# Rotary halves of queries and keys: 32 small transfers issued by ScalarE in place of eight permutation products on TensorE

## What is computed

```python
qkv = (x @ w_qkv).reshape(B, T, 3, H, Dh)
q = apply_rope(q, cos, sin) * (Dh ** -0.5)
k = apply_rope(k, cos, sin)

def apply_rope(t, cos, sin):
    t1, t2 = jnp.split(t, 2, axis=-1)
    return jnp.concatenate([t1 * cos - t2 * sin, t2 * cos + t1 * sin], axis=-1)

s_own = jnp.where(causal, einsum('bhqd,bhsd->bhqs', q_c, k_own), -jnp.inf)
p = softmax(s_own); out = (p @ v) @ w_o
```

## Time and profile before

| | us |
|---|---|
| median of 3 runs | 1294.86 (1294.64 to 1295.3) |
| the profiled execution | 1294.79 |
| its span | 1292.9 |
| TensorE busy | 1246.3 (96%) |
| VectorE busy | 902.7 (70%) |
| ScalarE busy | 641.3 (50%) |
| GpSimd busy | 69.7 (5%) |
| chain that ended last | PE 72%, DVE 19%, ACT 7%, issue 2% |

### The profile page before, as it was taken

One profiled execution on the slowest core, in us unless ns is written; L12 is line 12 of the kernel. 1 busy time (PEld: TensorE's weight loads), 2 busy tenths in 40 slices (PEclk: granted clock), 3 DMA queues, 4 the chain that ended last, 5 costly groups with the idle time before them and its releaser, 6 DMA issues.

```text
span 1292.9 us, 22010 instructions
## 1 busy us (share of the span) xinstructions
PE 1246.3 (96%) x9332; PEld 1087.3 (84%) x9332; DVE 902.7 (70%) x1433; ACT 641.3 (50%) x966; POOL 69.7 (5%) x43
## 2 busy tenths in 40 slices
PE   6999999999999999999999999999999999999997
PEld 4788898788888888768888889999898987788886
DVE  7456885766655677756665568989999766665555
ACT  3433445464554455556444445444455556555553
POOL 0022000002000061000200010000000000000000
PEclk9999999999999999999999999999999999999999
DMA  9532201665655374326555537455544343355550
GB/s 306 174 110 77 87 4 52 212 231 192 197 195 195 106 245 172 120 77 228 196 195 196 194 112 233 131 163 184 161 145 162 132 163 106 122 202 191 193 180 33
DMA packets 156211, 205.97 MB, mean 159 GB/s; under 512 B 9904, under 2 KB 129840, under 8 KB 155984
## 3 DMA queue, kind: packets, MB, share of 16 engines
q1 hardware_dynamic: 156112, 204.55, 47.9%
HBM read 202.44 MB, written 1.05 MB: 157 GB/s over the span
## 4 chain that ended last, share of the span: by engine, by line
PE 72%; DVE 19%; ACT 7%; issue 2%; DMA 0%; DVEq 0%; SPq 0%; ACTq 0%
PE PS L591 15%; PE PS L543 11%; PE PS L544 11%; PE PS L545 11%; PE PS L596 8%; DVE WW L2157 6%; PE PS L961 4%; DVE PH L2748 4%; ACT WW L1519 2%; PE PS L892 1%; DVE PA L2396 1%; PE PS L932 1%; ACT Xb L1555 1%; PE PS L668 1%; DVE PH L2766 1%
## 5 line engine op out<-in xcount | busy, mean ns | idle before, releaser
L2157 DVE TENSOR_TENSOR WW<-RG,WW 128x2048 fp32r<-128x2048 f32 x164 | 381.0, 2337 | 141.9 <-ACT WW L1519 141.7
L1519 ACT ACTIVATE WW<-RG 128x2048 fp32r<-128x2048 f32 x164 | 311.1, 1906 | 27.6 <-PE PS L545 24.8
L591 PE MATMUL PS<-AHL,WW 128*128 128x512 f32 x864 | 216.9, 392 | 0.4 <-DVE WW L2157 0.4
L543 PE MATMUL PS<-AHL,WW 128*128 128x256 f32 x704 | 203.3, 289 | 2.5 <-DVE AHL L2196 1.8
L544 PE MATMUL PS<-AHL,WW 128*128 128x256 f32 x704 | 199.1, 283 | 0.0
L545 PE MATMUL PS<-AHL,WW 128*128 128x256 f32 x704 | 199.1, 283 | 0.0
L591 PEld LDWEIGHTS PS<-AHL,WW 128*128 128x128 f32 x864 | 157.1, 189 | 30.0 <-DVE WW L2157 0.8
L543 PEld LDWEIGHTS PS<-AHL,WW 128*128 128x128 f32 x704 | 134.9, 192 | 5.3 <-issue 3.7
L544 PEld LDWEIGHTS PS<-AHL,WW 128*128 128x128 f32 x704 | 134.9, 192 | 1.7 <-issue 1.4
L545 PEld LDWEIGHTS PS<-AHL,WW 128*128 128x128 f32 x704 | 134.9, 192 | 0.0
L596 PEld LDWEIGHTS PS<-AHL,WW 128*128 128x128 f32 x864 | 118.4, 190 | 8.8
(11 more groups left out here) (369 smaller groups left out, 1837.7 us busy)
## 6 DMA issues: line engine op xcount, KB each, us to landing
RG<-in_ffn_w_in SPq DMA_DIRECT2D x44, 1024.0 KB, 5.3
RG<-in_w_ff SPq DMA_DIRECT2D x32, 1024.0 KB, 5.4
RG<-in_w_in SPq DMA_DIRECT2D x30, 1024.0 KB, 5.2
RG<-in_ffn_w_down SPq DMA_DIRECT2D x22, 1024.0 KB, 4.9
RG<-in_w_rkv SPq DMA_DIRECT2D x12, 1024.0 KB, 6.9
RG<-in_moba_w_qkv SPq DMA_DIRECT2D x12, 1024.0 KB, 7.9
RG<-in_w_o SPq DMA_DIRECT2D x4, 1024.0 KB, 8.0
RG<-in_wx_kv SPq DMA_DIRECT2D x4, 1024.0 KB, 5.7
```

Source lines behind the costliest of these rows:

```text
L543: e.matmul(o, lh, rh, start=start, stop=False)
L591: e.matmul(PS[b][:, :].rearrange("p (a t) -> p a t", a=2), wh, AHL[:, :, k * 256:k * 256 + 256], start=k == 0, stop=False)
L1519: s.activation(WH[hi_n % NW], ring(SPLIT[hi_n]), ACT.Copy, bias=0.0, scale=1.0).then_inc(s_hi, 1)
L2157: v.tensor_tensor(WL[lo_n % NW], ring(SPLIT[lo_n]), WH[lo_n % NW].bitcast(F32), ALU.subtract).then_inc(s_lo, 1)
```

## The change

The permutation product, its constant and its semaphore go. ScalarE, right after its copy to raw, waits for that copy to be finished and issues four transfers, each of 32 partitions by 512 elements, that bring the two halves of each of the two heads crosswise into `rot[u % 2]`, in the second half of Xb. VectorE's first operation reads `rot` in place of the PSUM bank and waits for its semaphore (four times 16 for each use). The sign is in the sine table. TensorE frees its banks by the copy to raw (`s_rw`) and no longer by the finished turn. ScalarE waits once, at u = 0, until the remainders of the old content of Xb are made, and once, before it rounds the third chunk of the output into XH, for all eight turns.

```diff
-               ('sel2', 2), ('pad', 14), ('perm', 128), ('cmask', 384), ('c01', 384), ('cos', 256), ('sin', 256)]:
+               ('sel2', 2), ('pad', 14), ('cmask', 384), ('c01', 384), ('cos', 256), ('sin', 256)]:
...
-    put('sin', np.tile(np.sin(ang), (4, 1)))
+    put('sin', np.where(p64 < 32, -1.0, 1.0) * np.tile(np.sin(ang), (4, 1)))
...
+        s_rot = [sem(f"rope_rotated{n}_in") for n in range(2)]
...
+        rot = [Xb[:, 1024 + 512 * n:1536 + 512 * n] for n in range(2)]
...
-            def rope_turn(u):
-
-                e.wait_ge(s_rw, u + 1)
-                e.matmul(PS[4 + u % 4][:, :], cst('perm'), raw[u % 2], start=True, stop=True).then_inc(s_pm, 1)
...
-                    rope_turn(5)
...
                     if u >= 4:
-                        e.wait_ge(s_rp, u - 3)
+                        e.wait_ge(s_rw, u - 3)
                     chan_piece(name, 4 + u % 4, 0)
                     if stepping:
                         step()
-                        if u != 6:
-                            rope_turn(u - 1)
                     chan_piece(name, 4 + u % 4, 1)
                     if stepping:
                         step()
-                    elif u:
-                        rope_turn(u - 1)
...
             moba_out(0, 0, (0, 1))
-            rope_turn(7)
+            e.wait_ge(s_rw, 8)
             moba_out(0, 0, (2, 3))
...
                 s.activation(raw[u % 2], PS[4 + u % 4][:, :], ACT.Copy, bias=0.0, scale=1.0).then_inc(s_rw, 1)
+                if u == 0:
+                    s.wait_ge(s_tl, H_AT['ln1'] + 4)
+                s.wait_ge(s_rw, u + 1)
+                for o_, i_ in ((0, 32), (32, 0), (64, 96), (96, 64)):
+                    s.dma_start(rot[u % 2][o_:o_ + 32, :], raw[u % 2][i_:i_ + 32, :]).then_inc(s_rot[u % 2], 16)
...
             s.wait_ge(s_oa, 6)
+            s.wait_ge(s_rp, 8)
             rounded(OTf, (2,), 1.0, XH)
...
-                v.wait_ge(s_pm, u + 1)
-                own_dve(v.tensor_tensor(d_, PS[4 + u % 4][:, :].rearrange("p (m t) -> p m t", m=2), sinb, ALU.mult))
+                v.wait_ge(s_rot[u % 2], 64 * (u // 2) + 64)
+                own_dve(v.tensor_tensor(d_, rot[u % 2].rearrange("p (m t) -> p m t", m=2), sinb, ALU.mult))
```

More of the change, by code:

```diff
@@ L58, in constants @@
     put('sel2', (p // 64) == np.arange(2)[None, :])
-    n_out, n_in = f % 64, p % 64
-    same = (p // 64) == (f // 64)
-    put('perm', np.where(same & (n_out < 32) & (n_in == n_out + 32), -1.0, 0.0)
-        + np.where(same & (n_out >= 32) & (n_in == n_out - 32), 1.0, 0.0))
     t1 = np.arange(256)[None, :] - 128
@@ L213, in build @@
         s_fg, s_fx, s_fhh, s_fhl, s_dn = (sem(n) for n in ("ffn_gate", "ffn_prod", "ffn_hi", "ffn_lo", "ffn_down_mm"))
-        s_rw, s_rc, s_pm, s_rp, s_v2 = (sem(n) for n in ("rope_raw", "rope_cos", "rope_mm", "rope_out", "moba_v"))
+        s_rw, s_rc, s_rp, s_v2 = (sem(n) for n in ("rope_raw", "rope_cos", "rope_out", "moba_v"))
+        s_rot = [sem(f"rope_rotated{n}_in") for n in range(2)]
         s_sc, s_mx, s_ex, s_pn, s_pt, s_pta, s_pv, s_oa = (sem(n) for n in (
```

## The result

The changed kernel takes 1308.97 us (median of 4 executions, 1308.12 to 1310.86), the kernel before 1295.08 on the same chip. The ratio is 1.0107, 95% interval 1.0095 to 1.0119: **slower by 13.9 us**, where +6.4 was forecast. The direction was right; the time lies 2.5 us above the range's upper end. Of the 13.9 us some 0.7 lie outside the span: 2.5 to 2.9 us in the four executions, where the kernel before has 1.9. One execution of the kernel before, taken beside **hybrid_tie** and **hybrid_fill5**, took 3169.91 us and enters no ratio.

What follows compares the result with a forecast made beforehand. Bound by TensorE and a ScalarE-VectorE loop of almost equal length. Shifts of +0.9, +2.9, +4.9, +5.0 (TensorE's scores), +7.3 and +6.4 through pieces 2 to 7 gave 1294.8 + 6.4 = 1301.2 us, range 1297.5 to 1306.5.

Steps and rivals of the forecast that it cites:

- 4 D - 1.6: Total shift in us for ScalarE's loss D per piece, said to hold as long as D is above 1.1.
- Two limits of almost the same length, and the change lengthens the loop: Rotary and attention stage: TensorE and a closed ScalarE-VectorE loop of 8.95 us per turn; issues fall inside that loop.
- TensorE's waits for the loop are just waits: Unstated: work behind TensorE's waits keeps its old time, so the last scores come 4.30 us after the output product starts.
- free-issue rival: ScalarE hands over a transfer in about 0.05 us, D = 0.2; -1.1 us, 1293.7; chance 0.10.
- the TensorE rival: TensorE is the only limit, the other loop has slack; eight product pairs go, -6.9 us, 1287.9; chance 0.06.
- D = 0.15 + 4 x 0.45 = 2.0: ScalarE's loss per piece: 0.15 us wait for its own copy, four issues of 0.45; bounds 1.7 and 3.0.
- u = 2, +0.9: Third of eight pieces (u = 0 to 7): copy 0.86 us earlier, VectorE's subtraction at 483.68 and not 482.78.
- Reading from SBUF in place of PSUM costs nothing: VectorE's first operation on the rotated half: both kinds of read take 0.69 us, so priced at nothing.
- Landings covered up to u = 6, exposed at u = 7: Landings of 2.2 us are hidden through piece 6; piece 7 is turned at 550.65, last scores at 550.85.
- the late landing: Rival at piece 7: transfers share engines with 1 MB loads and land in 7.9 us; 1306.7; chance 0.14.
- signs of being wrong in kind: TensorE without new gaps, VectorE waiting for a transfer at pieces 1 to 6, or time lost outside this stage.
- Nothing else moves: Behind the last scores +6.4 us stays to the end; time outside the span stays 1.9 us.

Runs made afterwards that it cites:

- hybrid_tie: Kernel before, with pieces 3 to 6 rotated by SyncE-issued transfers, VectorE subtracting the next piece before the exponentials, GpSimd's last product held back; 1293.60 us, 0.9985.
- hybrid_fill5: hybrid_tie plus five products that nothing reads in TensorE's wait ahead of the output product; 1292.36 us, 0.9977.
- issue_only: Changed kernel, all 32 transfers still issued by ScalarE, but VectorE takes the unrotated piece without waiting for landings; 1309.42 us, 1.0108.
- warm_tie: Changed kernel with unread products in three TensorE waits and GpSimd's last product held until VectorE's first remainder instruction ends; 1305.91 us, 1.0085.
- none: Changed kernel without any transfers or ScalarE's wait for its own copy; VectorE takes the unrotated piece; 1298.59 us, 1.0025.
- none_tie: none with GpSimd's last product held back until VectorE's first remainder instruction has ended; 1295.26 us, 0.9999.
- self_wait: none with ScalarE's wait for its own raw copy put back; 1297.46 us, 1.0020.

## Why the prediction was right in direction and wrong in size

The steps count D, what ScalarE loses at each piece, five times, at pieces 2 to 6. The formula 4 D - 1.6 that the prediction drew from them does not follow: shifting D in the steps gives 5 D - 3.6. The two agree at D = 2.0 alone. With D = 3.0 the steps give 11.4 and not 10.4, which puts even the highest D of the prediction close under its upper end. What fell short, in order of size: the size of D; the work behind TensorE's waits, taken at its old speed; and the collision at the last remainder, counted at nothing.

- *Two limits of almost the same length, and the change lengthens the loop.* Right. The turn grew by what ScalarE needs for its issues, the 0.12 for its own copy included, and by nothing else. TensorE has new waits, 3.11 and 2.38 us near where one of 4 was forecast, and 5.81 before the output product; 2.07 at 484.44 and 1.81 at 521.13 were not forecast. Of the other forecast places two were wrong: before the scores at 532.79 and the last ones at 558.88 TensorE waits for nothing. It was late itself by then.
- *TensorE's waits for the loop are just waits.* This is the step that was never stated and failed. The sum treats work behind a wait as taking its old time ("the last scores 4.30 later"). It took 6.66 us, 2.4 more, at half clock. Two experiments with fills bear it out, 2.35 us in the changed kernel, where this time falls to 4.28, and 3.5 without transfers, 1.3 of it in this place. For the same reason the free-issue rival's -1.1 and the -6.9 of the TensorE rival were both out of reach: free issues give +3.2.
- *D = 0.15 + 4 x 0.45 = 2.0.* Mis-sized. This is the largest part of what is missing, 4.5 of 8.1 us at the last scores. Measured over what the raw copy took before, D is 2.68 us at piece 2 and 3.35, 2.67, 3.09 and 2.68 at pieces 3 to 6 (rounding start less copy start less 0.48). The law is 0.12 + 4 x 0.64 = 2.68, and an issue that now and then takes 1.0 to 1.3 us does the rest. The two outputs at 0.50 were the wrong nearest rows. The 0.71 of the SBUF-to-SBUF issues, used for the upper bound alone, was the nearer one: the same kind of transfer and the same 64 KB. Its merged row also hides that one of the sixteen issues took 1.42 us; the median of the trace of before is 0.617 us, against 0.612 on ScalarE now. With it D would have been 0.15 + 4 x 0.62 = 2.6, and the steps give 9.4.
- *u = 2, +0.9.* +1.9. The copy of piece 2 started at 479.56, 0.3 later than forecast. From it to the rounding at 482.72 are 3.16 us and not 0.48 + 2.0, which is D again. VectorE's waits for the first landings have no part in it: VectorE stands idle for ScalarE's rounding just before the subtraction (0.28 us), and without those waits (**issue_only**) it comes at 484.55, with them at 484.66.
- *Reading from SBUF in place of PSUM costs nothing.* Right for VectorE's own time, 0.69 both ways.
- *Landings covered up to u = 6, exposed at u = 7.* The forecast that TensorE would meet piece 7 just after its turn held: VectorE waits 1.43 us for it at 554.11 and is done at 555.52, and TensorE comes to the scores at 558.88, having worked at half clock (552.22 + 4.30 = 556.52 without). The last transfer landed some 2 us after its issue, so the late landing, the rival nearest to the measured time, is not what happened. VectorE also waited for pieces 0 and 1. At piece 1 that is one of the prediction's own signs of being wrong in kind, but neither wait cost anything (**issue_only**).
- *Nothing else moves.* One thing did. GpSimd's last product started at 538.46, just behind VectorE's remainder at 538.42, and now starts at 550.27, just ahead of 550.29. The pair of remainder instructions takes 2.4 us both times, but now it is the first that is slowed and ends 1.1 us later, and the output product waits for it: it starts 1.93 us after the remainder's start, not 0.83. The Trainium skill ("SBUF — State Buffer", Who interferes with whom) says that a VectorE instruction with two inputs in SBUF contends with a GpSimd instruction that reads SBUF. The trace agrees, 2.39 us for the pair against 1.28 without the overlap, and whoever is first wins. A smaller thing is the time outside the span, taken as 1.9 us and measured at 2.5 to 2.9.

The terms, at the last scores of the profiled execution: 6.4 forecast, 1.35 + 0.67 + 1.09 + 0.68 = 3.8 for D, 1.0 at u = 2, 1.1 for the collision, 2.4 for the clock behind the last wait. Together 14.7, measured 14.5. The five D of this trace add up to 14.5, so 5 D - 3.6 gives 10.9; the late start of piece 2 (0.3), the collision and the clock are the rest. In **warm_tie**, where the last two are taken away, the five D add up to 13.95, so the turns alone give 10.4, and 10.8 was measured.

The Trainium skill's rule ("DMA: Bandwidth & Descriptors", Issuing engines are not separate DMA queues) that starting a DMA is usually cheap beside the DMA itself did not decide here. Each transfer lands 2.2 us (median) after its issue, so 0.61 is indeed the smaller part; but the landing is hidden, and the issue is on the path.

What stays open: why the clock fell in **none** and not in **none_tie** at the same place, some 0.7 us of what **none_tie** gained, why more time lies outside the span, and why some issues take 1.0 to 1.3 us.

## What to carry to other kernels

A DMA that replaces work on a busy engine is paid for on the engine that issues it, here per issue and not per byte: look for the issuer whose loop has slack, count the issues, and take the price from single issues of transfers of the same kind, not from a merged row. Where two loops are nearly equal, work taken from TensorE is a gain only if the other loop gets shorter too; otherwise it becomes a wait, and the work behind the wait can run slower. Shorten the loop first, then remove the product, and look at the clock behind each remaining wait.

## What was not expected of the hardware

- An issue of 64 KB and one of 32 KB both cost ScalarE 0.64 us from start to start; on GpSimd one takes 0.54.
- In **none** TensorE's clock was 0.68 from 505 to 510, behind a wait of 2.31 us, and 0.66 from 540 to 545, behind one of 3.13; it stayed at 1.00 in both where otherwise useless products filled the waits. Without permutation products, three traces of nearly one program (**none**, **self_wait**, **none_tie**) show different clocks from 500 to 510: 0.68 in the second half, 0.66 in the first, 1.00 in both. These kernels scatter by 2.6 to 3.9 us, the kernel before by 1.1 to 1.8. Its own mean clock is 0.995 to 0.999 from execution to execution, and 0.999 in the trace shown.
- At the remainder a few hundredths of a microsecond decide who is slowed. GpSimd started 0.04 us behind VectorE before and was the one to wait (its product took 1.79 us); in the changed kernel it started 0.02 us ahead, and VectorE waited. Holding back one GpSimd instruction, which nobody waits for there, was worth 1.1 us in the trace.
